# Order of work at the end of the second attention: sums, turned weights, loads of y and weight splits

## The chip, the cores and the metric

The kernel runs on one core of a Trainium2 chip. The metric is the device time of one execution in microseconds, median of three runs.

## The reference

A float32 stack of three layers over x of 512 tokens by 2048 features: a latent attention (mla, 16 heads), a sliding-window attention with sinks (swa, 32 query heads of 64, 4 key heads), and a stick-breaking attention beside a recurrence (stick). The change lies at the end of the second:

```python
proj = h @ w_in                       # q, k, v, gate
q, k = rope(q), rope(k)
s = where(valid, q k^T * D**-0.5, NEG_INF)      # own block of 128 keys and the one before
m = max(max(s), sink)
e = exp(s - m)
y = (e / (sum(e) + exp(sink - m))) @ v
x = x + (y * silu(gate)) @ w_out
```

Every large product is computed to nearly float32 precision: each operand is split into a high part (rounded, made by ScalarE) and a low part (the difference, made by VectorE or GpSimd), and PE sums high x high, high x low and low x high.

## The kernel before, in words

Tokens (512) stand in the free dimension, features in the 128 partitions. A weight tile is 2048 x 128 (1 MB), loaded by one DMA from SP's queue into one of two raw buffers, split in four pieces of 128 x 512 by `hi` (line 605, ScalarE) and `lo` (613, VectorE), and multiplied piece by piece by `multiply` (639 to 641, 12 matmuls a piece). `s_lo` counts pieces whose low part is made: a raw buffer is free for the next load when all four pieces of its tile are counted.

The phase swa runs 17 bodies. Body i projects the query tile and the gate tile of head pair i and does the attention of pair i - 1. Body 15 (`ends` in the code) still projects, body 16 (`not proj`) does only attention, and fills PE with the first tiles of the output projection out2: `early_output` (PE) multiplies piece p of tile (0, 0) and (0, 1) by turns, with chunks 4p to 4p + 3 of y as the other operand. The attention result of a pair leaves in two ways: for pairs up to 13 the turned weights go through a gather by DMA and are used a body later (`pv_prev`, "former pair"); bodies 15 and 16 turn the weights of their own pair on PE (`turn`, 1947 and 1951), copy them high (`turned_hi`, ScalarE) and low (`turned_lo`, VectorE, 658), and multiply (`pv`, 1981). Body 15 does both: the former pair's sums (`sum_prev`, 2196, counted as end_sum) must be out of a PSUM bank before `turn` may write it, and its `y_prev` and `y` share one buffer: `y` (2280) waits until the store of `y_prev` (732) has landed (`s_ystore`).

y goes to DRAM by one store a pair and comes back in four parts of up to four chunks (`load_y`, 741), each allowed once gate piece `part` of body 15 is multiplied. Then `y_hi` (1538, ScalarE) and `y_lo` (1548; VectorE, but chunks 4 to 7 GpSimd) split it. Chunk 15 is made in place by body 16's own `y`.

What sets the order around the change: each engine runs its instructions in the order in which `swa_T` (PE), `swa_A` (ScalarE), `swa_V` (VectorE), `swa_G` (GpSimd) and `attention_dmas` (SP) issue them; a wait blocks all behind it on that engine. The table `STEPS` (line 140 on) lists the counted steps of each engine, to turn a name into a semaphore value. In VectorE's body 15: maxima, inverse, this_lo(0), this_lo(1), q_cos, q_turn, q_sin, qr, this_lo(2), the four sums of the former pair, q_lo0, q_lo1, this_lo(3), y_prev, silu, the four low parts of the turned weights, next_lo(0), next_lo(1), sum_rows (2271), y, next_lo(2), next_lo(3). In body 16: y_lo 0 and 1, gate (2187), y_lo 2 and 3, first_lo(0), maxima (2161), inverse, first_lo(1), y_lo 8 to 11, first_lo(2), silu, turned_lo with first_lo(3) in their middle, y_lo 12 to 14, sum_rows, y, y_lo 15. this_lo is a piece of body 15's gate tile, next_lo one of out2's tile (0, 0), first_lo one of its tile (0, 1). SP's queue at the end of the phase: load tile (0, 0), load tile (0, 1) (when this_lo(3) is made), store y_prev, load y parts 0, 1, 2, store y of body 15, load tile (1, 0), y part 3, load tile (1, 1).

## Time and profile before

| | us |
|---|---|
| runs (3) | 2100.08, 2100.10, 2100.24; median 2100.1 |
| span of the profiled execution | 2098.9 |
| PE busy | 2082.9 (99%) |
| VectorE busy | 1417.7 (68%) |
| ScalarE busy | 996.4 (47%) |
| GpSimd busy | 191.2 (9%) |

The span runs from the first to the last instruction; the 1.2 us to the median lie around it. PE's clock was granted at 0.999 over the span. In all views PE is TensorE, DVE VectorE, ACT ScalarE, POOL GpSimd, SP the queue that issues the DMAs. Matmuls are pipelined, one of 512 columns starting every 0.23 us and listed with 0.39; an idle time is counted from the end of the one before. Consecutive operations of one kind are merged in a timeline (x4), and their time is then from the first start to the last end.

### The profile page before, as it was taken

To read this page: it belongs to the slowest core of one execution; us is meant where nothing else is said; L and a number is where in the kernel's file an instruction comes from. 1 tells how busy PE (TensorE), PEld (TensorE's weight loads), DVE (VectorE), ACT (ScalarE), POOL (GpSimd) and SP (SyncE) were. 2 spreads that over 40 slices of the span, in tenths; PEclk is the share of its full clock that TensorE was granted. 3 is DMA by queue.
4 is the path that set the end of the run, shared out by engine and by line. 5 is a ranking of instruction groups with operands and counts; after the bars stand their busy time and mean duration, and the time that the engine had idled before them with its cause. 6 is when DMAs were issued, how large, how long until landed. Compare 5 with 4: busy or idle time off the path is not lost. (4 is left out here: it accounts for less than half of the span.)

```text
span 2098.9 us, 30066 instructions
## 1 busy us (share of the span) xinstructions
PE 2082.9 (99%) x9702; PEld 1734.5 (83%) x9702; DVE 1417.7 (68%) x2581; ACT 996.4 (47%) x1928; POOL 191.2 (9%) x197
## 2 busy tenths in 40 slices
PE   9999999999999999999999999999999999999999
PEld 7888888888888888888888788888888888888887
DVE  6677777777733568888888633677777677868432
ACT  6444444445422446666666633544454545446221
POOL 0111111112101000000000122200000000003000
PEclk9999999999999999999999999999999999999999
DMA  7324444445733624444444734533434334345742
GB/s 227 100 72 113 111 112 114 113 114 170 210 83 97 196 63 122 126 127 127 127 127 118 250 95 115 170 106 86 121 101 133 87 108 119 109 114 156 218 112 70
DMA packets 409917, 264.40 MB, mean 126 GB/s; under 512 B 20480, under 2 KB 382720, under 8 KB 409856
## 3 DMA queue, kind: packets, MB, share of 16 engines
q1 hardware_dynamic: 401120, 255.87, 43.1%
q10 hardware_dynamic: 8736, 7.74, 1.5%
q8 instruction: 35, 0.57, 0.1%
q14 instruction: 26, 0.21, 0.0%
HBM read 210.33 MB, written 24.12 MB: 112 GB/s over the span
## 5 line engine op out<-in xcount | busy, mean ns | idle before, releaser
L639 PE MATMUL pp<-act_hi,w_hi 128*128 128x512 f32 x2304 | 903.1, 392 | 6.9 <-DVE w_lo L613 4.2
L641 PE MATMUL pp<-act_hi,w_lo 128*128 128x512 f32 x2304 | 898.2, 390 | 0.0
L640 PE MATMUL pp<-act_lo,w_hi 128*128 128x512 f32 x2304 | 897.9, 390 | 0.0
L613 DVE TENSOR_TENSOR w_lo<-raw,w_hi 128x512 fp32r<-128x512 f32 x680 | 457.1, 704 | 360.7 <-ACT w_hi L605 359.8
L605 ACT ACTIVATE w_hi<-raw 128x512 fp32r<-128x512 f32 (+1 forms) x684 | 396.2, 622 | 456.2 <-PE pp L641 231.3
L639 PEld LDWEIGHTS pp<-act_hi,w_hi 128*128 128x128 f32 x2304 | 433.1, 188 | 100.9 <-DVE w_lo L613 6.0
L641 PEld LDWEIGHTS pp<-act_hi,w_lo 128*128 128x128 f32 x2304 | 432.9, 188 | 91.1
L640 PEld LDWEIGHTS pp<-act_lo,w_hi 128*128 128x128 f32 x2304 | 433.2, 188 | 87.3 <-issue 0.2
L658 POOL TENSOR_TENSOR pT_lo<-gathered,pT_hi 128x640 fp32r<-128x640 f32 x30 | 46.5, 1571 | 358.9 <-ACT pT_hi L654 358.9
L1318 ACT ACTIVATE prob<-ps,minus,q_scale 128x512 f32<-128x512 f32 (+1 forms) x64 | 39.0, 615 | 78.3 <-DVE minus L1398 78.3
L639 PE MATMUL ps<-act_hi,w_hi 128*128 128x512 f32 x176 | 69.3, 394 | 0.0
L641 PE MATMUL ps<-act_hi,w_lo 128*128 128x512 f32 x176 | 68.5, 389 | 0.0
L640 PE MATMUL ps<-act_lo,w_hi 128*128 128x512 f32 x176 | 68.5, 389 | 0.0
L2045 ACT ACTIVATE s_prob<-ps,s_minus 128x256 f32<-128x256 f32 x96 | 44.7, 472 | 44.6 <-DVE s_minus L2161 44.6
L1705 POOL TENSOR_TENSOR acc<-acc,square 128x512 f32<-128x512 f32 x30 | 41.2, 1373 | 252.6 <-ACT square L1631 251.8
L1548 POOL TENSOR_TENSOR act_lo<-y_lru,act_hi 128x512 fp32r<-128x512 f32 x7 | 11.1, 1620 | 557.3 <-ACT act_hi L1538 557.3
L654 ACT ACTIVATE s_pT_hi<-gathered 128x1792 fp32r<-128x1792 f32 x14 | 23.9, 1705 | 72.2 <-DMA gathered<-turned 72.2
L2066 ACT ACTIVATE s_prob<-s_prob,s_inv 128x256 f32<-128x256 f32 x128 | 54.5, 503 | 0.0
L2161 DVE CUSTOM_DVE_ANT_0 ps<-ps,s_con,s_sink 128x256 f32<-128x256 f32 x96 | 47.4, 550 | 3.4 <-DVEq L2158 3.4
L1682 DVE TENSOR_TENSOR xT<-pp,xT 128x512 f32 (+1 forms) x28 | 19.3, 690 | 32.1 <-PE pp L641 32.1
L1901 DVE STREAM_TRANSPOSE turned<-s_prob 128x128 f32<-128x128 f32 (+1 forms) x56 | 32.8, 624 | 11.6 <-ACT s_prob L2066 11.6
L640 PEld LDWEIGHTS ps<-act_lo,w_hi 128*128 128x128 f32 x176 | 33.0, 188 | 7.3 <-issue 0.5
(435 smaller groups left out, 2755.1 us busy)
## 6 DMA issues: line engine op xcount, KB each, us to landing
raw<-w_in SPq DMA_DIRECT2D x48, 1024.0 KB, 5.9
raw<-swa_w_in SPq DMA_DIRECT2D x36, 1024.0 KB, 5.8
raw<-mla_w_in SPq DMA_DIRECT2D x23, 1024.0 KB, 5.7
raw<-mla_w_out SPq DMA_DIRECT2D x16, 1024.0 KB, 6.5
raw<-swa_w_out SPq DMA_DIRECT2D x16, 1024.0 KB, 6.1
raw<-w_out SPq DMA_DIRECT2D x16, 1024.0 KB, 6.9
gathered<-turned SPq DMA_DIRECT2D x224, 56.0 KB, 2.0
x_feature_major<-xT SPq DMA_DIRECT2D x8, 1024.0 KB, 9.7
```

Source lines behind the costliest of these rows:

```text
L605: q.eng.activation(dst, raw_piece(tile, p), ACT.Copy).then_inc(s_hi, tile.ups(p))
L613: q.eng.tensor_tensor(dst, raw_piece(tile, p), high, ALU.subtract).then_inc(s_lo, tile.ups(p))
L639: q.eng.matmul(psum[:, :], wh, ah, start=start and n == 0, stop=False)
L640: q.eng.matmul(psum[:, :], wh, al, start=False, stop=False)
L641: last = q.eng.matmul(psum[:, :], wl, ah, start=False, stop=stop and n == PIECE // P - 1)
L658: q.eng.tensor_tensor(out, in_, hi_part.bitcast(F32), ALU.subtract).then_inc(*q.did(step))
L1318: q.eng.activation(prob[:, OFF[b]:OFF[b] + w_], SCORE[b][:, 0:w_], ACT.Exp, bias=minus[:, b:b + 1], scale=q_scale[:, b:b + 1], accum_out=t ...
L1705: q.eng.tensor_tensor(into, into, src[:, k, :], ALU.add).then_inc(*q.did(f"sum{f}{k}"))
L1901: m = q.eng.transpose(out_, in_)
L2045: q.eng.activation(s_prob[:, h, b * 2 * P:(b + 1) * 2 * P], BANKS[h][half][:, b % 2 * 2 * P:(b % 2 + 1) * 2 * P], ACT.Exp, bias=s_minus[:, ...
L2066: m = q.eng.activation(pr, pr, ACT.Identity, scale=s_inv[:, h, b:b + 1])
L2161: m = q.eng.tensor_tensor_reduce(scores, scores, sc("band")[:, b * 2 * P - half * 2 * P:(b + 1) * 2 * P - half * 2 * P], s_q_scale[:, b:b ...
```

## The change

In body 15, VectorE makes the former pair's sums right behind the shuffle `q_turn`, then this_lo(2), q_sin and qr, then the four low parts of the turned weights (now counted as end_lo), then this_lo(3), and then the query's low parts, y_prev, silu, next_lo(0), sum_rows, y, next_lo(1). ScalarE copies the turned weights (end_hi) ahead of the query's high parts. Pieces 2 and 3 of tile (0, 0) are split in body 16: behind y_hi 1 on ScalarE and behind y_lo 1 on VectorE. In body 16 first_lo(1) goes ahead of inverse(1), and first_lo(3) behind all four low parts of the turned weights. SP loads y parts 0 and 1 ahead of tile (0, 1) and of the store of y_prev. The arithmetic, the number of instructions and the bodies 0 to 14 stay.

```diff
--- before.py
+++ after.py
@@ -139,10 +139,10 @@
     },
     "swa": {
         "T": "s00 s01 s10 s11 pv_prev0 pv_prev1 t00 t01 t10 t11 pv0 pv1".split(),
-        "A": ("exp00 exp01 exp02 exp03 sink0 exp10 exp11 exp12 exp13 sink1 norm0 norm1 tanh low_prev0 low_prev1 q_hi0 q_hi1 "
-              "turned_hi pt_hi00 pt_hi01 pt_hi10 pt_hi11 y_low0 y_low1").split(),
-        "V": ("gate ready0 minus00 minus01 ready1 minus10 minus11 sum0 inv0 lo_prev sum1 inv1 turned q_cos q_turn q_sin qr "
-              "end_sum00 end_sum01 end_sum10 end_sum11 q_lo0 q_lo1 sum_prev00 sum_prev01 sum_prev10 sum_prev11 y_prev silu pt_lo00 pt_lo01 pt_lo10 pt_lo11 "
+        "A": ("exp00 exp01 exp02 exp03 sink0 exp10 exp11 exp12 exp13 sink1 norm0 norm1 tanh low_prev0 low_prev1 "
+              "end_hi00 end_hi01 end_hi10 end_hi11 q_hi0 q_hi1 turned_hi pt_hi00 pt_hi01 pt_hi10 pt_hi11 y_low0 y_low1").split(),
+        "V": ("gate ready0 minus00 minus01 ready1 minus10 minus11 sum0 inv0 lo_prev sum1 inv1 turned q_cos q_turn "
+              "end_sum00 end_sum01 end_sum10 end_sum11 q_sin qr end_lo00 end_lo01 end_lo10 end_lo11 q_lo0 q_lo1 sum_prev00 sum_prev01 sum_prev10 sum_prev11 y_prev silu pt_lo00 pt_lo01 pt_lo10 pt_lo11 "
               "y_sum00 y_sum01 y_sum10 y_sum11 y").split(),
         "G": "sink keys pair".split(),
     },
@@ -772,10 +772,13 @@
             load_tile(q.eng, Tile(f"out{n}", 0, 0))
             if phase == "mla":
                 gather(units - 1)
+            else:
+                load_y(q, n, 0)
+                load_y(q, n, 1)
             load_tile(q.eng, Tile(f"out{n}", 0, 1))
             if phase == "swa":
                 store_y(q, phase, units - 1, units - 3, "V.y_prev")
-            for part in range(3):
+            for part in range(0 if phase == "mla" else 2, 3):
                 load_y(q, n, part)
             store_y(q, phase, units - 1, units - 2)
             if n == 1:
@@ -1970,7 +1973,7 @@
             def pv():
 
                 if not proj or ends:
-                    q.eng.wait_ge(*q.at("V.pt_lo11"))
+                    q.eng.wait_ge(*q.at("V.end_lo11" if ends else "V.pt_lo11"))
                     q.eng.wait_ge(*q.at("G.pair", i))
                     hi_, lo_ = (pT[:, :].rearrange("p (h n) -> p h n", h=2) for pT in (s_pT_hi, s_pT_lo))
                     for half, parts in enumerate((((0, 0, 0, 2), (1, 2, 1, 1)), ((2, 5, 0, 2), (1, 3, 0, 1), (3, 4, 1, 1)))):
@@ -2081,9 +2084,17 @@
             def turned_hi(h, half):
                 if not proj or ends:
                     q.eng.wait_ge(*q.at(f"T.t{h}{half}"))
-                    copy_hi(q, turned_blocks(s_pT_hi, h, half), TURNED[h][half][:, half * P:], f"pt_hi{h}{half}")
+                    copy_hi(q, turned_blocks(s_pT_hi, h, half), TURNED[h][half][:, half * P:], f"{'end' if ends else 'pt'}_hi{h}{half}")
+
+            def all_turned():
+                for h in range(2):
+                    for half in range(2):
+                        turned_hi(h, half)
             if not proj:
-                y_hi(q, 2, range(0, 4))
+                y_hi(q, 2, range(0, 2))
+                hi(q, Tile("out2", 0, 0), 2)
+                hi(q, Tile("out2", 0, 0), 3)
+                y_hi(q, 2, range(2, 4))
                 hi(q, Tile("out2", 0, 1), 0)
                 y_hi(q, 2, range(4, 8))
             weights(0, 0)
@@ -2110,23 +2121,20 @@
             this_hi(3)
             if not proj:
                 hi(q, Tile("out2", 0, 1), PIECES - 1)
+            if ends:
+                all_turned()
             if proj:
                 q.eng.wait_ge(*q.at("V.qr"))
                 copy_hi(q, s_q_a[0:HD2, :], s_q[0:HD2, :], "q_hi0")
                 copy_hi(q, s_q_b[HD2:P, :], s_q[HD2:P, :], "q_hi1", rest=not attn)
             if ends or not proj:
-                turned_hi(0, 0)
-                turned_hi(0, 1)
-                turned_hi(1, 0)
-                turned_hi(1, 1)
                 next_hi(0)
                 next_hi(1)
                 if not proj:
+                    all_turned()
                     y_hi(q, 2, range(12, KC - 1))
                 low_rows(0)
                 low_rows(1)
-                next_hi(2)
-                next_hi(3)
                 return
             next_hi(0)
             next_hi(1)
@@ -2172,14 +2180,17 @@
 
             def turned_lo(h, half):
                 if not proj or ends:
-                    q.eng.wait_ge(*q.at(f"A.pt_hi{h}{half}"))
+                    name = "end" if ends else "pt"
+                    q.eng.wait_ge(*q.at(f"A.{name}_hi{h}{half}"))
                     sub_lo(q, turned_blocks(s_pT_lo, h, half), TURNED[h][half][:, half * P:], turned_blocks(s_pT_hi, h, half),
-                           f"pt_lo{h}{half}")
+                           f"{name}_lo{h}{half}")
             def first_lo(p):
                 if not proj:
                     lo(q, Tile("out2", 0, 1), p)
             if not proj:
                 y_lo(q, 2, range(0, 2))
+                lo(q, Tile("out2", 0, 0), 2)
+                lo(q, Tile("out2", 0, 0), 3)
             if attn:
                 multiplied(q, Tile("swa", i - 1, 1))
                 if not isinstance(i, int) or i >= 2:
@@ -2204,8 +2215,8 @@
             if prev:
                 q.eng.wait_ge(*q.at("A.turned_hi", i - 1))
                 sub_lo(q, s_pT_lo[:, :], gathered[:, :], s_pT_hi[:, :], "lo_prev")
+            first_lo(1)
             inverse(1)
-            first_lo(1)
             if not proj:
                 y_lo(q, 2, range(8, 12))
             first_lo(2)
@@ -2225,21 +2236,30 @@
                     q.eng.wait_ge(*q.at("V.q_lo1", i - 1))
                 q.eng.tensor_tensor(s_q[:, :], pp[0][:, :], s_cos[:, :], ALU.mult).then_inc(*q.did("q_cos"))
                 q.eng.stream_shuffle(s_spin, pp[0][:, :], PARTNER).then_inc(*q.did("q_turn"))
+                if ends:
+                    sum_prev(0)
+                    sum_prev(1)
+                    this_lo(2)
                 q.eng.wait_ge(*q.at("V.q_turn"))
                 q.eng.tensor_tensor(s_spin, s_spin, s_sin[:, :], ALU.mult).then_inc(*q.did("q_sin"))
                 q.eng.wait_ge(*q.at("V.q_sin"))
                 q.eng.tensor_tensor(s_q[:, :], s_q[:, :], s_spin, ALU.add).then_inc(*q.did("qr"))
-            this_lo(2)
             if ends:
-                sum_prev(0)
-                sum_prev(1)
+                turned_lo(0, 0)
+                turned_lo(0, 1)
+                turned_lo(1, 0)
+                turned_lo(1, 1)
+                this_lo(3)
+            else:
+                this_lo(2)
             if proj:
                 q.eng.wait_ge(*q.at("A.q_hi0"))
                 sub_lo(q, s_q_a[HD2:P, :], s_q[0:HD2, :], s_q_a[0:HD2, :], "q_lo0")
                 q.eng.wait_ge(*q.at("A.q_hi1"))
                 q.eng.tensor_tensor(s_q_b[0:HD2, :], s_q[HD2:P, :], s_q_b[HD2:P, :].bitcast(F32),
                                     ALU.subtract).then_inc(*q.did("q_lo1", rest=not attn))
-            this_lo(3)
+            if not ends:
+                this_lo(3)
             if prev:
                 if not ends:
                     sum_prev(0)
@@ -2253,15 +2273,14 @@
                 q.eng.wait_ge(*q.at("A.tanh"))
                 q.eng.scalar_tensor_tensor(s_y[:, 1, :], s_th[:, :], 1.0, s_gate, ALU.add,
                                            ALU.mult).then_inc(*q.did("silu", rest=proj and not ends))
-            turned_lo(0, 0)
-            turned_lo(0, 1)
-            first_lo(3)
-            turned_lo(1, 0)
-            turned_lo(1, 1)
             if ends:
                 next_lo(0)
-                next_lo(1)
             if not proj:
+                turned_lo(0, 0)
+                turned_lo(0, 1)
+                turned_lo(1, 0)
+                turned_lo(1, 1)
+                first_lo(3)
                 y_lo(q, 2, range(12, KC - 1))
             def sum_rows(half):
                 if not proj or ends:
@@ -2279,9 +2298,11 @@
                 q.eng.wait_ge(*q.at("V.y_sum11"))
                 q.eng.scalar_tensor_tensor(s_y[:, 0, :] if proj else last_y, s_y_sum[:, :], 0.5, s_y[:, 1, :],
                                            ALU.mult, ALU.mult).then_inc(*q.did("y"))
-            if not ends:
-                next_lo(0)
+            if ends:
                 next_lo(1)
+                return
+            next_lo(0)
+            next_lo(1)
             next_lo(2)
             next_lo(3)
```

## Rows read from the trace of the kernel before

**Rows 1.** The page, engine shares: busy us (share of the span) xinstructions.

```profile
PE 2082.9 (99%) x9702; PEld 1734.5 (83%) x9702; DVE 1417.7 (68%) x2581; ACT 996.4 (47%) x1928; POOL 191.2 (9%) x197
```

**Rows 2.** Waits of PE, whole span: engine line <- waited for: total us, times, longest.

```profile
PE pp L639 <- DVE w_lo L613: 4.2, 4, 2.0
```

**Rows 3.** Timeline of PE, restarts: start us, us, operation, [idle before <-releaser].

```profile
1149.63 0.33 PE L1947 MATMUL pt<-con,s_prob 128*128 128x128 f32 x1 [1.10 <-DVE s_y_sum L2196]
...
1155.13 0.49 PE L1981 MATMUL po<-s_pT_hi,pair 128*128 128x512 f32 x1 [1.01 <-DVE s_pT_lo L658]
...
1163.46 0.47 PE L639 MATMUL pp<-act_hi,w_hi 128*128 128x512 f32 x1 [1.78 <-DVE act_lo L1548]
...
1167.58 0.47 PE L639 MATMUL pp<-act_hi,w_hi 128*128 128x512 f32 x1 [0.76 <-DVE w_lo L613]
...
1174.24 0.50 PE L639 MATMUL pp<-act_hi,w_hi 128*128 128x512 f32 x1 [0.97 <-DVE w_lo L613]
...
1183.35 0.50 PE L1981 MATMUL po<-s_pT_hi,pair 128*128 128x512 f32 x1 [0.39 <-DVE s_pT_lo L658]
...
1188.95 0.50 PE L639 MATMUL pp<-act_hi,w_hi 128*128 128x512 f32 x1 [0.28 <-DVE act_lo L1548]
```

**Rows 4.** Timeline of ACT, 1144 to 1152.

```profile
1144.91 1.08 ACT L2073 ACTIVATE s_y_low<-pt 64x512 f32<-64x512 f32 x2
...
1150.38 0.98 ACT L654 ACTIVATE s_pT_hi<-pt 128x512 fp32r<-128x512 f32 x2 [1.77 <-PE pt L1947]
```

**Rows 5.** Timeline of DVE, 1145 to 1160.

```profile
1145.10 0.74 DVE L2227 STREAM_SHUFFLE square<-pp 128x512 f32<-128x512 f32 x1
...
1147.82 1.75 DVE L2196 TENSOR_TENSOR s_y_sum<-pt,s_y_low 64x256 f32<-64x256 f32 x4
...
1150.92 0.70 DVE L613 TENSOR_TENSOR w_lo<-raw,w_hi 128x512 fp32r<-128x512 f32 x1
...
1152.86 1.15 DVE L658 TENSOR_TENSOR s_pT_lo<-pt,s_pT_hi 128x512 fp32r<-128x512 f32 x2
...
1157.70 0.87 DVE L2271 TENSOR_TENSOR s_y_sum<-ps,s_y_low 64x256 f32<-64x256 f32 x2
...
1158.67 0.69 DVE L2280 SCALAR_TENSOR_TENSOR s_y<-s_y_sum,s_y 128x512 f32<-128x512 f32 x1
...
1159.28 1.29 DVE L613 TENSOR_TENSOR w_lo<-raw,w_hi 128x512 fp32r<-128x512 f32 x2
```

**Rows 6.** DMA issues: xcount, KB each, us to landing; windows at 1151.6, 1152.2, 1153.5; whole span.

```profile
raw<-swa_w_out SPq DMA_DIRECT2D x1, 1024.0 KB, 6.2
...
y_feature_major<-s_y SPq DMA_DIRECT2D x1, 256.0 KB, 6.3
...
y_whole<-y_feature_major SPq DMA_DIRECT2D x1, 1024.0 KB, 8.4
...
y_feature_major<-y_out SPq DMA_DIRECT2D x15, 256.0 KB, 2.2
```

**Rows 7.** Timeline of POOL, 1165 to 1172.

```profile
1165.39 1.49 POOL L1548 TENSOR_TENSOR act_lo<-y_whole,act_hi 128x512 fp32r<-128x512 f32 x1 [21.41 <-ACT act_hi L1538]
...
1166.85 1.73 POOL L1548 TENSOR_TENSOR act_lo<-y_whole,act_hi 128x512 fp32r<-128x512 f32 x1
...
1171.03 0.39 POOL L2310 CAST pair<-s_v_hi 128x256 fp32r<-128x256 f32 x1
```

**Rows 8.** Timeline of DVE, 1165 to 1168 and at 1914.

```profile
1165.64 1.80 DVE L613 TENSOR_TENSOR w_lo<-raw,w_hi 128x512 fp32r<-128x512 f32 x1
...
1167.36 0.54 DVE L2161 CUSTOM_DVE_ANT_0 ps<-ps,s_con,s_sink 128x256 f32<-128x256 f32 x1
...
1914.36 2.89 DVE L613 TENSOR_TENSOR w_lo<-raw,w_hi 128x512 fp32r<-128x512 f32 x2
```

**Rows 9.** Timeline of ACT, 1173 to 1181.

```profile
1173.00 1.71 ACT L2066 ACTIVATE s_prob<-s_prob,s_inv 128x256 f32<-128x256 f32 x4
...
1179.85 0.97 ACT L654 ACTIVATE s_pT_hi<-pt 128x512 fp32r<-128x512 f32 x2
```

## The prediction, made before the changed kernel ran

> **What bounds the kernel now.** Read the page's engine shares first: PE (TensorE) is busy 2082.9 of 2098.9 us [rows 1], so all its idle time together is 16 us, and no edit of order can gain more. The list of waits by PE then says what ends that idle time: above all VectorE's low parts of weights, 4.2 us in 4 waits [rows 2]. The edit touches only the last attention unit with projections (I call it unit 15) and the drain after it (unit 16), so the third view is PE's timeline there: seven restarts between 1149.6 and 1189.0, whose marked idle times 1.10, 1.01, 1.78, 0.76, 0.97, 0.39 and 0.28 add up to 6.29 us [rows 3]. That is the ceiling: 0.30% of the time. A measurement of this kernel can tell about 0.2%, 4.2 us, from no change.
>
> Which of the seven can be had is not PE's affair. The last one, output chunk 15 at 1188.95 [rows 3], needs the drain's own attention result. Behind it lies a chain from VectorE's first maximum at 1167.36 [rows 8] over ScalarE, which is busy without a break from its normalisation at 1173.00 to the high parts at 1179.85 [rows 9], back to VectorE and PE. From the maximum to chunk 15 it is 1188.95 - 1167.36 = 21.6 us. PE's own work from its restart at 1167.58 to chunk 15 is 21.37 less the idle 0.97, 0.39 and 0.28, so 19.7 us [rows 3]. The chain is longer by 1.9 us or so: **the end follows the moment at which unit 16's maxima start on VectorE**, and stalls of PE after 1167 cost nothing by themselves. So the sum is the shift of that moment.
>
> **Part 1: sums ahead in unit 15.** The four sums (1.75 us [rows 5]) move from behind qr and a weight split to behind the shuffle, which ends at 1145.84 [rows 5]; the low rows that they read are there at 1144.91 + 1.08 = 1145.99 [rows 4] (the first about half of that earlier). They end near 1147.5, not 1149.57. PE wants the bank at 1149.63 - 1.10 = 1148.5 [rows 3]: the 1.10 go. What is late next: nothing until the product.
>
> **Part 2: turned weights ahead of the query's parts.** The turns finish 1.26 sooner (start 1148.4), ScalarE's four copies, which began at 1150.38 [rows 4], begin at 1149.1. Their four low parts need 2.2 us (first pair at 1152.86, 1.15 for two, the second pair alike [rows 5]), from 1149.7 to 1151.9; PE comes to the product at about 1153.0 (1155.13 - 1.01 - 1.10 [rows 3]). The 1.01 go. The cover has 1 us of room.
>
> What they are moved past pays: the weight split this_lo(3), ended at 1150.92 + 0.70 = 1151.62 [rows 5], now follows the four low parts: 1151.9 + 0.6 = 1152.5. The query's low parts (2 x 0.7), y_prev (0.7), silu (0.7) and next_lo(0) (0.6) follow: y_prev ends near 1154.55, next_lo(0) near 1155.9. The sums of the product (2 x 0.87 [rows 5]) end at 1157.6 instead of 1158.57. PE, after the product and the fourth gate piece and scores, is ready for output chunk 0 near 1159.5 (1163.46 - 1.78 - 2.11 [rows 3]).
>
> **Part 3: y's DMAs, and the wait that stays.** The two loads of y go out when gate pieces 0 and 1 are through (about 1145.9 and 1148.6) and land before 1155; one took 8.4 us only behind other transfers [rows 6]. The 1.78 us wait thus loses its cause. But SP's queue still holds, in this order, the tile load out2(0,1), which waits for this_lo(3), and the store of y_prev; and VectorE's "y" waits until that store has landed, since it overwrites its buffer. Before: the tile load went out as this_lo(3) ended, 1151.62, and took 6.2 us to land [rows 6]: 1157.8; the store, issued 0.6 later, took 6.3 [rows 6]: about 1158.5; y started at 1158.67 [rows 5], so this wait was already a tie with the sums. After: this_lo(3) ends 1152.5, the tile lands at 1152.55 + 6.2 = 1158.8, the store 0.7 later, 1159.5. **y starts at 1159.5, 0.8 later than before**, though its inputs are there at 1157.6. Behind y queue on VectorE next_lo(1), all of unit 16, and PE's chunks.
>
> What of the store's landing the trace doesn't settle: the same 256 KB with nothing ahead took 2.2 us (y_out, 15 of them [rows 6]), which would be 1156.8 and no wait; behind a tile it took 6.3. I take the latter, as the order in the queue is the same as in that row. The Trainium skill ("DMA: Bandwidth & Descriptors", Queues, rings and completion order) says the completion write lands only after every earlier write of that DMA engine; by it the 2.2 us is not to be had with the tile ahead, and the 0.7 us between the landings agrees.
>
> **Part 4: splits moved in the drain.** Between y's end (1160.2) and the maxima VectorE now has nine operations: next_lo(1), y_lo 0 and 1, splits 2 and 3 of out2(0,0), gate, y_lo 2 and 3, first_lo(0). At 0.6 each (two take 1.29 [rows 5]) the maxima would start at 1160.1 + 5.4 = 1165.5, a gain of 1.85. But **GpSimd** runs y_lo 4 to 7 meanwhile. In the trace of before its first (1.49 us from 1165.39) held up w_lo, which then took 1.80 instead of 0.69, and w_lo its second, 1.73 instead of 1.49; the operation on PSUM after it took 0.54 [rows 7, 8]. At 1914 two w_lo beside such work took 2.89 instead of 1.29 [rows 8]. So they take turns: each w_lo or y_lo waits for GpSimd's operation and the other way round, a pair costing about 1.7 us where VectorE alone needs 0.6. In before, ScalarE's y_hi 4 came so late that only one VectorE operation met this (1.11). Now y_hi 4 follows hi(out2(0,1), 0), which waits for the tile at 1158.8; GpSimd begins at about 1160.05, just as y ends, and four VectorE operations meet its four: next_lo(1), y_lo 0, y_lo 1, split 2, each +1.1. The first of its two casts (0.39 each [rows 7]) delays split 3 by some 0.3. Sum 4 x 1.1 + 0.3 = 4.7: maxima at 1165.5 + 4.7 = 1170.2. Chunk 0 on PE at 1163.7 (before 1163.46), chunks 2 and 3 only near 1169.2, the next tile at 1170.5.
>
> **Ends of that price.** Below: no turns at all, 0, if GpSimd is the one that waits. Above: all eight port-using operations held, 8 x 1.1 = 8.9, which four GpSimd operations can't do. I take 4.7, by the count of meetings. The Trainium skill ("SBUF — State Buffer", SBUF: two separate sides) says whoever starts first holds the pair for the whole instruction and a VectorE operation is concerned when it has two SBUF inputs. It doesn't say who is next when both queue; read as "a running VectorE queue keeps it" the time would be that of rival B. The rows at 1165 and 1914 speak for turns.
>
> **first_lo(1) ahead of inverse(1)** takes PE's 0.97 stall away, first_lo(3) behind the four low parts most of the 0.39: both lie beside the 21.6 us chain, so 0. The cover is the chain itself; if the maxima came 2 us sooner relative to PE, they would count. next_hi(2), (3) move into ScalarE's idle time. The split 2, 3 later delay the tile load of out2(1,0) to near 1167.9; it is needed after 1188.
>
> **Sum.** Maxima 1170.2 - 1167.36 = +2.8 us, and 21.6 us behind them unchanged: chunk 15 at 1191.8. Span 2098.9 + 2.8 = 2101.7. Before, the median 2100.1 is 1.2 above the span; so 2102.9 us, 0.13% more.
>
> **Rivals.** A is this forecast, chance 0.62 (2101.5 to 2104.2 by half a microsecond either way at the landing and one meeting more or less).
> B, faster: VectorE is not held. Maxima at 1165.5, 2098.3 us. For it: an operation can slip between two of GpSimd's; against it the turns at 1165 and 1914 [rows 7, 8]. 0.20.
> C, slower for sure: the tile out2(0,1) lands later because the two loads of y stand ahead of it in the queue. A load of the same size behind two others took 8.4 us to land where the tile took 6.2 [rows 6]: 2.2 more. Everything behind y then shifts by that on top of the 2.8: 2105.1. It passes +4.2 once the tile lands 1.4 later than I put it, after 1160.2. Against: the second load is issued 4 us ahead. 0.10.
> D: the store lands in time. Then y at 1157.7, two or three operations get ahead of GpSimd, the rest meet it: maxima near 1167.9, 2100.6 us. 0.05.
> E: the edit does more than I count, as where neither the wait nor the turns bite: y at 1157.7 and 5.4 us behind it, maxima at 1163.7, 2096.4. 0.03.
>
> **Numbers.** Range 2097.8 to 2104.6: B to the upper end of A, leaving out C and E, 0.15 or so. Faster by over 0.2% (below 2095.9): 0.03. Slower (above 2104.3): 0.12. Within: 0.85.
>
> **What would show it.** After: no idle ahead of the first turn and the first product in unit 15; y_whole landed before 1155; y's start 0.1 us behind the landing of the y_prev store and the sums' end 2 us before; w_lo and y_lo of 1.1 to 1.8 us just behind y, beside GpSimd's 1.7; maxima near 1170. Wrong if y starts at 1157.7, if these VectorE operations last 0.69, or if the distance from maxima to chunk 15 is not 21.6.

## The result, and the profile after

| | before | after |
|---|---|---|
| median of nine runs each, us | 2100.24 (2099.43 to 2101.05) | 2105.16 (2104.12 to 2108.72) |
| ratio to before | | 1.0024, 95% interval 1.0015 to 1.0032 |
| span of the profiled execution | 2098.9 | 2102.3 (its time 2104.12, the lowest of the nine) |

The changed kernel is slower by 4.9 us. The forecast was 2.8 us slower, and the time lies 0.6 us above the range. A second set of eleven runs (last experiment) gave 2104.89, 3.8 us above its own runs of before, so the size is 3.8 to 4.9 us.

The page, engine shares of after: busy us (share of the span) xinstructions.

```profile
PE 2084.9 (99%) x9702; PEld 1736.4 (83%) x9702; DVE 1420.5 (68%) x2581; ACT 995.3 (47%) x1928; POOL 192.4 (9%) x197
```

PE is *busy* for 2.0 us longer than in [rows 1] with the same 9702 matmuls, and VectorE for 2.8 us longer with the same 2581 instructions. Neither engine got work. Both facts belong to the answer: matmuls at a lower clock, and subtractions held up by GpSimd's. A third part of it, VectorE's wait for a store, is idle time and shows in neither.

Waits of PE in after, whole span: engine line <- waited for: total us, times, longest.

```profile
PE pp L639 <- DVE act_lo L1551: 7.8, 3, 5.7
PE pp L639 <- DVE w_lo L613: 2.4, 2, 1.9
```

The waits for w_lo fell from the 4.2 of [rows 2] to 2.4, as intended. A wait of 5.7 us for the low part of y stands in their place. Timeline of PE in after, the restarts: start us, us, operation, [idle before <-releaser].

```profile
1147.41 0.60 PE L1950 MATMUL pt<-con,s_prob 128*128 128x128 f32 x4
...
1151.68 0.39 PE L1984 MATMUL po<-s_pT_hi,pair 128*128 128x512 f32 x1
...
1163.83 0.77 PE L639 MATMUL pp<-act_hi,w_hi 128*128 128x512 f32 x1 [5.73 <-DVE act_lo L1551]
...
1168.22 0.80 PE L639 MATMUL pp<-act_hi,w_hi 128*128 128x512 f32 x1 [1.16 <-DVE act_lo L1551]
...
1185.87 0.50 PE L1984 MATMUL po<-s_pT_hi,pair 128*128 128x512 f32 x1 [0.16 <-DVE s_pT_lo L658]
...
1192.06 0.50 PE L639 MATMUL pp<-act_hi,w_hi 128*128 128x512 f32 x1 [0.90 <-DVE act_lo L1551]
```

The first turn and the first product no longer wait: the 1.10 and 1.01 of [rows 3] are gone. But output chunk 0 waits 5.73, and the matmul behind it lasts 0.77 instead of 0.47.

To compare absolute times of two traces, a common mark is needed. I take the shuffle of unit 15, which in before starts at 1145.10 [rows 5]. Timeline of VectorE in after:

```profile
1144.14 0.73 DVE L2238 STREAM_SHUFFLE square<-pp 128x512 f32<-128x512 f32 x1
...
1159.12 1.23 DVE L2299 SCALAR_TENSOR_TENSOR s_y<-s_y_sum,s_y 128x512 f32<-128x512 f32 x1 [2.46 <-DMA y_feature_major<-s_y]
1160.27 1.75 DVE L613 TENSOR_TENSOR w_lo<-raw,w_hi 128x512 fp32r<-128x512 f32 x1
1161.94 3.42 DVE L1551 TENSOR_TENSOR act_lo<-y_whole,act_hi 128x512 fp32r<-128x512 f32 x2
1165.28 1.68 DVE L613 TENSOR_TENSOR w_lo<-raw,w_hi 128x512 fp32r<-128x512 f32 x2
...
1169.29 0.54 DVE L2169 CUSTOM_DVE_ANT_0 ps<-ps,s_con,s_sink 128x256 f32<-128x256 f32 x1
```

and of POOL in the same stretch:

```profile
1158.53 6.28 POOL L1551 TENSOR_TENSOR act_lo<-y_whole,act_hi 128x512 fp32r<-128x512 f32 x4 [15.52 <-ACT act_hi L1541]
1164.76 0.85 POOL L2331 CAST pair<-s_v_hi 128x256 fp32r<-128x256 f32 x1
```

After's clock stands 0.96 us earlier than before's at the mark, so after's maxima at 1169.29 are 1170.25 in the time of before. y waited 2.46 us until the store of y_prev had landed, and then ran against GpSimd: y 1.23, next_lo(1) 1.75, two y_lo 3.42 together.

DMA issues of after, 1144.5 to 1161: xcount, KB each, median us to landing.

```profile
y_whole<-y_feature_major SPq DMA_DIRECT2D x3, 1024.0 KB, 5.5
raw<-swa_w_out SPq DMA_DIRECT2D x1, 1024.0 KB, 5.8
```

The first two loads of y, issued at 1144.92 and 1147.67, land at 1150.37 and 1153.20, well ahead of any need. The tile goes out at 1151.52 and lands at 1157.28; the store goes out at 1153.68 and lands at 1159.09.

The last view shows what I had not looked for. Windows of before and then of after: us, busy time and instructions of each engine, PEclk the granted clock, DMA share, GB/s.

```profile
1160.00:1165.00 5.00, 3.22 (x21) 2.53 (x19) 2.94 (x5) 3.04 (x6) 0.00 (x0) 1.00 1.04 387
1165.00:1170.00 5.00, 4.15 (x18) 3.09 (x18) 4.82 (x12) 3.42 (x11) 4.61 (x4) 1.00 1.05 311
```

```profile
1155.00:1160.00 5.00, 3.10 (x22) 2.70 (x20) 2.45 (x5) 4.91 (x10) 1.47 (x2) 1.00 1.03 346
1160.00:1165.00 5.00, 1.17 (x3) 0.83 (x3) 5.00 (x4) 0.01 (x1) 5.00 (x4) 0.72 0.16 62
1165.00:1170.00 5.00, 3.84 (x9) 2.33 (x8) 5.00 (x10) 0.00 (x0) 1.42 (x2) 0.50 0.29 82
1170.00:1175.00 5.00, 5.00 (x18) 3.97 (x17) 4.06 (x17) 4.61 (x20) 0.00 (x0) 0.76 0.92 286
```

PE's clock, 1.00 in every one of these windows before, fell to 0.50, that is from 2.4 to 1.2 GHz, while PE idled ahead of chunk 0. It stayed there for (0.28 + 0.50 + 0.24) x 2 x 5 = 10.2 us. The next view shows it in the matmuls: they start 0.43 apart instead of 0.23.

```profile
1168.81 0.63 PE L640 MATMUL pp<-act_lo,w_hi 128*128 128x512 f32 x1
1169.23 0.63 PE L641 MATMUL pp<-act_hi,w_lo 128*128 128x512 f32 x1
```

Fifteen of them start 0.43 instead of 0.23 apart. The first six cost nothing, as PE waited 1.16 us for the low part of y behind them anyway; the nine from 1168.22 on put PE 9 x 0.2 = 1.8 us further behind. It then came late with the second turn of unit 16, on which ScalarE and, behind it, VectorE wait. ACT timeline of after at 1184:

```profile
1184.03 0.98 ACT L654 ACTIVATE s_pT_hi<-ps 128x512 fp32r<-128x512 f32 x2 [1.29 <-PE ps L1950]
```

and the DVE timeline behind it:

```profile
1184.65 1.16 DVE L658 TENSOR_TENSOR s_pT_lo<-ps,s_pT_hi 128x512 fp32r<-128x512 f32 x2 [1.10 <-ACT s_pT_hi L654]
```

From the maxima to chunk 15 it is 1192.06 - 1169.29 = 22.8 us, not 21.6.

**Where the time went, profiled run against profiled run.** Maxima later against the mark: (1169.29 - 1144.14) - (1167.36 - 1145.10) = 2.9 us. Chain behind them: 22.77 - 21.59 = 1.2. Rest of the span behind chunk 15: (2102.3 - 1192.06) - (2098.9 - 1188.95) = 0.3. Together 4.4. Up to the mark after was 0.96 faster, in code that the change doesn't touch, so the spans differ by 3.4 only. The medians, where such offsets wash out, differ by 4.9.

### The profile page after: what moved, and what is told of

It is laid out like the page before. It is cut to its first block, busy times and chain, and to the rows that moved or that the text cites. A ratio compares the mean times of both kernels' runs of the same rounds, so it can differ in the third digit from the quotient of the medians.

```text
span 2102.3 us, 30095 instructions
## 1 busy us (share of the span) xinstructions
PE 2084.9 (99%) x9702; PEld 1736.4 (83%) x9702; DVE 1420.5 (68%) x2581; ACT 995.3 (47%) x1928; POOL 192.4 (9%) x197
## 4 chain that ended last, share of the span: by engine, by line
PE 93%; DVE 4%; ACT 1%; DMA 1%; issue 1%; ACTq 0%; SPq 0%; DVEq 0%
PE pp L639 25%; PE pp L640 25%; PE pp L641 25%; PE ps L639 2%; PE ps L641 2%; PE ps L640 2%; PE ps L662 2%; PE ps L664 2%; PE ps L663 2%; DVE w_lo L613 1%; PE po L662 1%; PE po L664 1%; PE po L663 1%; PE pt L1967 1%; PE pt L1969 1%
```

## The experiments

All but two start from the changed kernel. They are told in the order of what they settle. The following table is read from their traces: y's start and the maxima's are counted from the shuffle; "shift" is (maxima plus chain) against before's 43.85; the last column is worked out from windows as above; "time" is the median against the runs of before beside it. Four kernels (both of these, loads of y back, loads of y alone, sums and turned weights alone) ran on another chip than the other six, beside runs of before with a median of 2100.47; the others stood beside 2100.91, or 2101.09 for splits back and after again. So across these groups the differences from before are the ones to compare.

| kernel | y | maxima | chain to chunk 15 | shift | time | us at 1.2 GHz near chunk 0 |
|---|---|---|---|---|---|---|
| before | 13.57 | 22.26 | 21.59 | | | 0 |
| after | 14.98 | 25.15 | 22.77 | +4.1 | +4.9 | 10.2 |
| after again | 15.96 | 26.29 | 22.30 | +4.7 | +3.8 | 10.2 |
| y in a buffer of its own | 12.55 | 21.71 | 21.58 | -0.6 | +0.5 | 3.4 |
| GpSimd later | 14.62 | 20.64 | 21.62 | -1.6 | -1.0 | 0 |
| both of these | 12.51 | 18.54 | 21.59 | -3.7 | -4.0 | 0 |
| store ahead of the tile | 12.57 | 18.59 | 21.63 | -3.6 | -3.5 | 0 |
| PE filled | 14.60 | 25.37 | 21.62 | +3.1 | +4.8 | 0 |
| loads of y back | 14.60 | 23.85 | 21.59 | +1.6 | +2.5 | 3.4 |
| loads of y alone | 14.63 | 23.82 | 21.59 | +1.6 | -0.2 | 0 |
| sums and turned weights alone | 14.52 | 22.57 | 21.59 | +0.3 | +0.6 | 6.8 |
| splits back | 14.96 | 24.73 | 21.60 | +2.5 | +2.7 | 6.8 |

A shift is that of one execution and a time that of a whole set. The profiled executions of own buffer, GpSimd later and PE filled were the lowest of their sets, that of loads alone the second highest; there the two columns part by 0.6 to 1.8 us.

### The wait alone: y in a buffer of its own

```diff
-                if proj:
-                    q.eng.wait_ge(s_ystore, 16 * (H1 - 1 + i))
...
-                q.eng.scalar_tensor_tensor(s_y[:, 0, :] if proj else last_y, ...
+                q.eng.scalar_tensor_tensor(s_q[:, :] if proj else last_y, ...
```

The store of this y reads s_q too.

> The changed kernel, but unit 15's y goes to a buffer of its own (the query's, free by then), so it doesn't wait until the store of y_prev has landed. Theory (the wait and the turns with GpSimd set the maxima, the end follows them): y starts at about 1156.7 instead of 1159.1, two more VectorE operations get ahead of GpSimd, the maxima start near 1166.9 instead of 1169.3, time 2105.2 - 2.4 = 2102.8 us, and 1.2 less again if TensorE's clock stays at 2.4 GHz. Rival (the lower clock of TensorE after its idle time is what costs, VectorE's delays are covered): the maxima move but the time stays within 1 us of 2105.2 as long as the clock falls. Rival (the wait is a tie that other work covers): no change.

Measured: 2101.45 (2099.50 to 2103.42), ratio 1.0004 (0.9995 to 1.0013): no difference from before can be told any more, and it is 3.7 us below after. y starts with its inputs at 1156.98, and six of the nine operations behind it get through before GpSimd begins at 1161.03. DVE timeline of this kernel:

```profile
1156.98 0.69 DVE L2298 SCALAR_TENSOR_TENSOR s_q<-s_y_sum,s_y 128x512 f32<-128x512 f32 x1
...
1161.20 3.33 DVE L1552 TENSOR_TENSOR act_lo<-y_whole,act_hi 128x512 fp32r<-128x512 f32 x2
1164.46 1.76 DVE L613 TENSOR_TENSOR w_lo<-raw,w_hi 128x512 fp32r<-128x512 f32 x1
```

and its POOL timeline:

```profile
1161.03 6.33 POOL L1552 TENSOR_TENSOR act_lo<-y_whole,act_hi 128x512 fp32r<-128x512 f32 x4 [17.71 <-ACT act_hi L1542]
```

So the wait was real and 2.4 us long, and the last three operations are still held. That only three are held is in part due to this execution, the lowest of its eleven: the tile took 8.0 us to land here, 5.8 in after, and GpSimd, which starts behind it, began 2.2 us later against the mark. With a sooner tile more of them would meet GpSimd; the median, 2.0 us above this execution, fits that but has no trace.

### The turns alone: GpSimd later

```diff
             if not proj:
+                q.eng.wait_ge(*q.at("V.ready0"))
                 y_lo(q, 2, Y_GPSIMD[2])
```

> The changed kernel with one wait more: GpSimd's four y_lo begin only when VectorE has come to unit 16's maxima. Theory (turns at the shared port cost 4.7 us): y and the eight operations behind it last 0.69 each, the maxima start 6.0 us behind y, near 1165.1 instead of 1169.3, chunk 15 follows 21.6 behind; time 2105.2 - 5.4 = 2099.8 us, or 2101.0 if the clock still falls. Rival (the turns are covered by PE's lower clock or by DMAs): less than 1 us faster. Rival (GpSimd's chunks 4 to 7 are then late for PE): a new idle time ahead of them, over 1 us.

Measured: 2099.91 (2098.10 to 2102.33), ratio 0.9998 (0.9989 to 1.0007), 5.3 us below after and 0.1 from the theory's 2099.8. y still waits for its store, but all behind it runs undisturbed. DVE timeline of this kernel:

```profile
1158.73 0.69 DVE L2299 SCALAR_TENSOR_TENSOR s_y<-s_y_sum,s_y 128x512 f32<-128x512 f32 x1 [2.15 <-DMA y_feature_major<-s_y]
1159.34 0.68 DVE L613 TENSOR_TENSOR w_lo<-raw,w_hi 128x512 fp32r<-128x512 f32 x1
1159.94 1.29 DVE L1551 TENSOR_TENSOR act_lo<-y_whole,act_hi 128x512 fp32r<-128x512 f32 x2
...
1164.75 0.55 DVE L2169 CUSTOM_DVE_ANT_0 ps<-ps,s_con,s_sink 128x256 f32<-128x256 f32 x1
```

From y to the maxima it is 1164.75 - 1158.73 = 6.02 us for ten operations; in after the same ten took 1169.29 - 1159.12 = 10.17. The turns cost 4.15 us. PE's idle ahead of chunk 0 was 2.75 and the clock stayed at 2.4 GHz.

### Both: own buffer and GpSimd later

The two diffs above in one kernel.

> The changed kernel with both: unit 15's y in a buffer of its own (no wait for the store) and GpSimd's four y_lo held until VectorE has come to the maxima. Theory (wait and turns are all that delays the maxima): y starts at about 1157 as its sums are there, the maxima 6.0 us behind it, near 1163, chunk 15 another 21.6 behind; 2.0 us faster than with either alone, 2097.9 us. Rival (with the maxima so early something else ends the stretch, the tile's landing at 1159 ahead of first_lo(0) or PE's own 19.7 us): maxima near 1163 but less than 1 us gained over the kernel with GpSimd held alone.

Measured: 2096.46 (2096.08 to 2098.23), ratio 0.9982 (0.9973 to 0.9991). It is 4.0 us below its before; after was 3.8 to 4.9 above, so taking both causes away is worth 7.8 to 8.9 us. That is 1.4 us better than the theory had: it built on the median of GpSimd later, which lies 1.8 us above the execution with the trace. The maxima come 18.54 after the mark, 6.6 sooner than in after: 2.5 from y's start and 4.15 from the turns. For the maxima, the two causes add up and leave nothing over.

### One line of SP's order: store ahead of the tile

```diff
                 load_y(q, n, 1)
+                store_y(q, phase, units - 1, units - 3, "V.y_prev")
             load_tile(q.eng, Tile(f"out{n}", 0, 1))
-            if phase == "swa":
-                store_y(q, phase, units - 1, units - 3, "V.y_prev")
```

> The changed kernel with the store of y_prev ahead of the load of tile (0, 1) in SP's queue. Theory (the store lands late only because the tile stands ahead of it): it lands in 2.2 us, y starts near 1156.7 as soon as its sums are there; the tile lands 2.2 us later, which also holds GpSimd back until 1160.8; maxima near 1166.0 instead of 1169.3, time 2105.2 - 3.3 = 2101.9 us, 2100.7 if the clock stays up. Rival (a store takes 5 to 6 us by itself): y still at 1159, the tile later, time 2105 to 2107. Rival (PE then lacks tile (0, 1)): idle time ahead of its first piece, no gain.

Measured: 2097.38 (2096.74 to 2098.55), ratio 0.9984 (0.9975 to 0.9993): it beats both kernels too, and lies 3.3 us below the better of the two times that the theory allowed. The theory had GpSimd held back only until 1160.8 and most of the turns still there. DMA issues of this kernel, window at 1154.8 to 1155.5:

```profile
raw<-swa_w_out SPq DMA_DIRECT2D x1, 1024.0 KB, 7.0
y_feature_major<-s_y SPq DMA_DIRECT2D x1, 256.0 KB, 3.0
```

The store lands in 3.0 us instead of 5.4, so y doesn't wait. The tile goes out 2.5 us later against the mark, takes 7.0 us instead of 5.8 and lands at 1162.36; GpSimd, which needs it by way of ScalarE, begins only at 1163.61, when VectorE is in its last operation ahead of the maxima. DVE timeline:

```profile
1157.99 0.69 DVE L2298 SCALAR_TENSOR_TENSOR s_y<-s_y_sum,s_y 128x512 f32<-128x512 f32 x1
...
1163.41 0.69 DVE L613 TENSOR_TENSOR w_lo<-raw,w_hi 128x512 fp32r<-128x512 f32 x1
```

POOL timeline:

```profile
1163.61 5.41 POOL L1550 TENSOR_TENSOR act_lo<-y_whole,act_hi 128x512 fp32r<-128x512 f32 x4 [19.37 <-ACT act_hi L1540]
```

One move takes away both costs. It also shows how they were coupled. GpSimd begins 1.25 us after the tile's landing (1158.53 against 1157.28 in after, 1163.61 against 1162.36 here, 1161.03 against 1159.77 with the own buffer), and y 0.03 after the store's. Behind one another in SP's queue, tile and store land within 2 us of each other, so **the same two landings release VectorE and GpSimd together**. The Trainium skill ("DMA: Bandwidth & Descriptors", Queues, rings and completion order) has a completion land only after every earlier write of its DMA engine; 5.4 us behind the tile and 3.0 ahead of it agree with that.

### The clock alone: PE filled

```diff
             scores(1, 1)
+            if not proj:
+                for _ in range(24):
+                    q.eng.matmul(pp[0][:, :], s_q_a[:, 0:P], pairk_hi[:, :], start=True, stop=True)
```

> The changed kernel with 24 matmuls more, whose results nothing uses, on PE between unit 16's scores and output chunk 0, where PE was idle for 5.7 us; they need 5.5 us. Theory (the clock's fall costs the 1.2 us by which chunk 15 came later behind the maxima than 21.6): if the clock stays at 2.4 GHz, maxima unchanged near 1169.3, chunk 15 at maxima + 21.6 instead of 22.8, time 2104.0 us. Rival (the clock costs all that PE's slower matmuls add, 15 of them at 0.43 instead of 0.23 us): 3 us faster, 2102.2. Rival (the clock falls anyway, by the pauses between the chunks): no change.

Measured: 2105.69 (2103.05 to 2108.00, eight runs), ratio 1.0025 (1.0014 to 1.0035). The matmuls only keep PE at work between the scores and chunk 0. Windows of the profiled execution:

```profile
1160.00:1165.00 5.00, 4.50 (x20) 3.44 (x19) 5.00 (x4) 0.64 (x2) 5.00 (x4) 1.00 0.21 80
1165.00:1170.00 5.00, 2.50 (x11) 1.41 (x10) 5.00 (x7) 0.00 (x0) 2.15 (x3) 1.00 0.13 34
```

The maxima, on VectorE:

```profile
1170.02 0.54 DVE L2172 CUSTOM_DVE_ANT_0 ps<-ps,s_con,s_sink 128x256 f32<-128x256 f32 x1
```

and the last two restarts of PE:

```profile
1185.45 0.50 PE L1984 MATMUL po<-s_pT_hi,pair 128*128 128x512 f32 x1 [0.97 <-DVE s_pT_lo L658]
...
1191.64 0.50 PE L639 MATMUL pp<-act_hi,w_hi 128*128 128x512 f32 x1 [0.88 <-DVE act_lo L1551]
```

The clock was 1.00 throughout and the chain from maxima to chunk 15 back at 21.62 us, although the maxima came as late as in after. In this execution that ties the extra 1.2 us to the clock. The median does not bear it out: the theory had 2104.0, and it did not fall. The two executions with a mean clock of 1.000 took 2103.05 and 2103.67; the six with 0.997 to 0.999 took 2105.20 to 2108.00. The filler may thus have failed to hold the clock in most executions. That isn't shown: only one has a trace, a mean over the span doesn't say where the clock fell, and runs of before have 0.998 to 1.000 too. The split by clock agrees in sign with the trace, though its 3 us are more than 1.2.

### Loads of y back behind the tile and the store

```diff
             load_tile(q.eng, Tile(f"out{n}", 0, 0))
-            else:
-                load_y(q, n, 0)
-                load_y(q, n, 1)
             load_tile(q.eng, Tile(f"out{n}", 0, 1))
-            for part in range(0 if phase == "mla" else 2, 3):
+            for part in range(3):
```

> The changed kernel with SP's queue as before: both loads of y behind the tile and the store. Theory (the maxima are set by the store's landing and the turns, not by y's loads): the first load of y lands at 1162 to 1163 instead of 1151, so ScalarE's y_hi 0 and VectorE's y_lo 0 wait until then; next_lo(1) is out of the way by then and GpSimd starts near 1166, so that one or two VectorE operations meet it instead of four: y_lo 0 near 1163.5, maxima near 1169.5, time 2105 within 1 us. Rival (the loads of y were the gain of the change): 2 us slower or more, 2107. Rival (they do harm, as they bring GpSimd into VectorE's stretch): faster than 2104.

Measured: 2102.94 (2101.65 to 2105.10), ratio 1.0014 (1.0005 to 1.0023). This was a miss for my theory, which gave the loads no part in the slowdown. With them back, VectorE waits 2.04 us for y instead of for GpSimd, GpSimd begins only at 1166.47 and holds one operation. DVE timeline:

```profile
1162.78 1.29 DVE L1548 TENSOR_TENSOR act_lo<-y_whole,act_hi 128x512 fp32r<-128x512 f32 x2 [2.04 <-ACT act_hi L1538]
...
1167.00 1.79 DVE L613 TENSOR_TENSOR w_lo<-raw,w_hi 128x512 fp32r<-128x512 f32 x1
```

The loads sooner thus take away a 2 us wait and open the door for a 4 us one: they are 1.3 to 2.4 us of the slowdown, by letting GpSimd start with y.

### Loads of y alone, on the kernel before

```diff
             load_tile(q.eng, Tile(f"out{n}", 0, 0))
+            else:
+                load_y(q, n, 0)
+                load_y(q, n, 1)
             load_tile(q.eng, Tile(f"out{n}", 0, 1))
...
-            for part in range(3):
+            for part in range(0 if phase == "mla" else 2, 3):
```

> The kernel before with only SP's queue changed as in the change: the two loads of y ahead of the tile and the store. Theory: y_lo 0 no longer waits for its load (idle 2.1 us on VectorE gone), GpSimd starts near 1162 and meets y_lo 2, y_lo 3 and first_lo(0) instead of first_lo(0) alone (2.2 us more); the maxima start 1 us sooner to 1 us later than in the kernel before, time 2100.1 +- 1. Rival (sooner loads are a plain gain): 2 us faster. Rival (turns eat more than the wait gives): 1 to 3 us slower.

Measured: 2100.31 (2099.21 to 2103.05), ratio 1.0001 (0.9992 to 1.0010). In the profiled execution, one of the slower (its time was 2102.77), GpSimd began at 1161.86 and held four operations, and the tile took 7.4 us to land; SP took 3.43 us to issue the store of y_prev, where 0.36 is usual, and it landed 7.5 us after its issue. SP timeline:

```profile
1152.20 3.43 SPq L732 DMA_DIRECT2D y_feature_major<-s_y  x1
```

Seven of the eleven runs lie below 2101, so most executions probably didn't look like this one. Alone the loads make no difference that the interval, 1.9 us either way, can tell; their harm comes with the other edits.

### Sums and turned weights alone, on the kernel before

```diff
+                if ends:
+                    sum_prev(0)
+                    sum_prev(1)
+                    this_lo(2)
                 q.eng.wait_ge(*q.at("V.q_turn"))
...
+            if ends:
+                turned_lo(0, 0)
+                turned_lo(0, 1)
+                turned_lo(1, 0)
+                turned_lo(1, 1)
+                this_lo(3)
```

and end_hi on ScalarE, as in the change; SP's order and the splits as before.

> The kernel before with only the sums of the former pair and the turned weights of unit 15 moved ahead; SP's queue and all weight splits of out2 as before. Theory (this_lo(3) ends 0.9 us later, and with it the tile's and the store's landings, y and the loads of y behind them): PE's idle times of 1.10 and 1.01 us go, but the maxima come 0.9 us later, time 0.9 us slower than before. Rival (PE's idle times are what counts): 2.1 us faster. Rival (the wait for the store doesn't move): no change.

Measured: 2101.10 (2100.52 to 2104.53), ratio 1.0006 (0.9997 to 1.0015), +0.6 us where parts 1 to 3 of the prediction gave +0.9. PE timeline of this kernel, ahead of chunk 0:

```profile
1163.01 0.76 PE L639 MATMUL pp<-act_hi,w_hi 128*128 128x512 f32 x1 [4.34 <-DVE act_lo L1548]
```

The 2.1 us won ahead of the turn and the product reappear as idle ahead of chunk 0 (1.78 before [rows 3], 4.34 here), and the clock was at 1.2 GHz for 6.8 us. It still cost nothing in the chain, 21.59.

### Splits back

```diff
-                y_hi(q, 2, range(0, 2))
-                hi(q, Tile("out2", 0, 0), 2)
-                hi(q, Tile("out2", 0, 0), 3)
-                y_hi(q, 2, range(2, 4))
+                y_hi(q, 2, range(0, 4))
```

and likewise in VectorE's list, with first_lo(1) and first_lo(3) where they were.

> The changed kernel with its weight splits where they were before: pieces 2 and 3 of out2(0,0) at the end of body 15, first_lo(1) behind inverse(1), first_lo(3) in the middle of the turned weights. Sums, turned weights and the loads of y stay as changed. Theory: the harm comes from GpSimd's four subtractions beginning with y, and they are released by the tile out2(0,1) on ScalarE, not by these splits; VectorE has the same nine operations between y and the maxima. So GpSimd begins within 0.5 us of y, four operations of VectorE last 1.7 us, maxima to chunk 15 is 21.6 us if the clock holds and up to 22.8 if PE's idle ahead of chunk 0 (longer here, as three pieces stand ahead of y_lo 0 on VectorE) lets it fall: 2104.5 to 2106 us. Rival: the moved splits are what pushes VectorE late; without the moves it is near the kernel with the sums and turned weights alone, 2101 to 2102 us.

Measured: 2103.75 (2102.57 to 2104.94), ratio 1.0012 (1.0003 to 1.0021), between the two theories: 0.75 us below mine and 1.75 above the rival's. GpSimd did begin with y (1159.19 and 1159.36). The moved splits are worth 1.1 to 2.3 us of the slowdown, against none in my theory. PE's idle ahead of chunk 0 was longest of all here. PE timeline:

```profile
1166.16 0.77 PE L639 MATMUL pp<-act_hi,w_hi 128*128 128x512 f32 x1 [7.36 <-DVE act_lo L1551]
```

and two windows, with the clock:

```profile
1160.00:1165.00 5.00, 0.00 (x0) 0.00 (x0) 5.00 (x4) 0.67 (x2) 5.00 (x4) 0.79 0.21 79
1165.00:1170.00 5.00, 3.84 (x10) 3.06 (x11) 5.00 (x9) 0.00 (x0) 2.07 (x3) 0.53 0.91 251
```

The low clock ended here at about 1169.7, 0.6 us behind the maxima at 1169.13; the chain is 21.60. In after it lasted 3.1 us past the maxima, and the chain grew by 1.2; in the second profile of after 2.1 us past them, and it grew by 0.7. Half speed hurts as far as it reaches into the time in which PE must catch up with the chain.

### The changed kernel once more

> The changed kernel itself, once more, for a second profiled execution and more times. Theory: y again within 0.5 us of the store's landing, GpSimd within 0.7 us of y, four VectorE operations of 1.7 us, maxima near 1169.3, the granted clock at 0.5 for some microseconds after PE's idle of over 5 us, maxima to chunk 15 over 22 us; median 2105.2, within 0.8. Rival: the profiled low clock of 10.2 us was a single case and the next execution shows 21.6 us; then the median stays at 2105 all the same and the clock is not part of it.

Measured: 2104.89 (2103.79 to 2106.63), ratio 1.0021 (1.0012 to 1.0030). The profiled execution took 2106.34, 2.2 us above the first one. DVE timeline:

```profile
1161.82 0.69 DVE L2299 SCALAR_TENSOR_TENSOR s_y<-s_y_sum,s_y 128x512 f32<-128x512 f32 x1 [3.48 <-DMA y_feature_major<-s_y]
1162.43 0.68 DVE L613 TENSOR_TENSOR w_lo<-raw,w_hi 128x512 fp32r<-128x512 f32 x1
1163.03 3.44 DVE L1551 TENSOR_TENSOR act_lo<-y_whole,act_hi 128x512 fp32r<-128x512 f32 x2
1166.40 3.43 DVE L613 TENSOR_TENSOR w_lo<-raw,w_hi 128x512 fp32r<-128x512 f32 x2
```

and the DMA issue of the tile:

```profile
raw<-swa_w_out SPq DMA_DIRECT2D x1, 1024.0 KB, 8.0
```

Here the tile took 8.0 us to land, not 5.8, and y started 1.0 later against the mark. Of the 4.7 us by which chunk 15 shifted here, 4.0 lie in the maxima and 0.7 in the chain. Among the profiled kernels with the loads of y and the tile in after's order, the tile took 5.8 to 6.2 us in five and 7.4 to 8.0 in three (own buffer, loads alone and this one); in the three with the loads behind it, 6.0 to 6.2. So this is rival C, in some executions only.

## Why the prediction was wrong

**Right.** The sums and the turned weights did what parts 1 and 2 say. The wait for the store of y_prev took over (y 0.03 us behind the landing, in both profiles), and VectorE and GpSimd took turns. The maxima stood at +2.9 us; the forecast was +2.8. The tests took each of the two causes away alone and together. Each set against its own before, and these against after's +3.8 to +4.9, the wait is worth 3.3 to 4.4 us, the turns 4.8 to 5.9 and both 7.8 to 8.9. So these two are shown, not only argued.

**Right by two errors that cancel.** In the time of before, y started at 1159.12 + 0.96 = 1160.1, not 1159.5. The failed step is "the store 0.7 later" than the tile. I took the distance of the two landings from before, where the issues were 0.6 apart. After the change y_prev is done later and they are 2.2 apart, and the landings 1.8. The prediction itself had y_prev end at 1154.55, 2.0 us behind its issue of the tile, and didn't use it. The tile landed 0.6 sooner than forecast, which hid part of that. Against that the turns cost 4.15, not 4.7: GpSimd started before y, so y took one of the four meetings, at +0.5 only. That the maxima came out at +2.8 and +2.9 was luck; in the second profile they came at +4.0.

**Wrong: "stalls of PE after 1167 cost nothing by themselves".** This is the step that failed in both profiles of after. It compared PE's work (19.7 us) with the chain (21.6) and kept 1.9 us of slack, at full clock. The change lengthened the idle ahead of chunk 0 to 5.7 us. PE's clock then fell to 1.2 GHz for 10.2 us, its matmuls ate the slack, and the chain took 22.8: +1.2 us (+0.7 in the second profile). The slack that could take up a delay was also smaller than 1.9. With the clock up (PE filled) the idle times of that stretch are 0.97 ahead of the product and 0.88 ahead of chunk 15. In after they are 0.16 and 0.90: only the first shrank, since the second waits for what VectorE makes of the product itself. Of the 1.9 us that PE's work took longer from its restart ahead of the maxima (22.8 instead of 20.8 us without the idle times) 0.8 was covered and 1.2 came through, within 0.1. My own text had the numbers for the idle: it put chunk 0 at 1163.7 and PE's readiness at 1159.5, 4 us apart, and never asked what an idle of that size does. In [rows 3] nothing is longer than 1.78, and there the clock never fell. The evidence for this step is three traces (both of after, and PE filled); no median shows it, as filling PE did not lower the time.

**Wrong: rival C as an either-or.** Its 2.2 us came true in size (8.0 against 5.8) but in some executions only. Where it did, in the second profile, y started 1.0 later and the maxima term was 1.2 us too small, more than the chain's 0.7. That the median lies 1 us above the first profiled execution, the lowest of its nine, fits this, but is only argued: just two executions have a trace. Why the tile takes 2 us longer in some executions and not in others wasn't settled: the loads of y ahead of it are a condition by the rows above, not yet a cause.

**Not in the sum.** Behind chunk 15 the profiled spans differ by another 0.3 us. And the base: I put 1.2 us around the span, median against the span of one execution. Time less span is 1.8 in a run (2104.12 - 2102.3), so the profiled execution of before probably lay 0.6 above the median itself.

**The gain that was missed.** Rival E had 2096.4 for the case that neither the wait nor the turns bite. The kernel with both taken away came to 2096.46, with its maxima at 18.54 from the mark, which is 1163.6 in the time of before; rival E had 1163.7. The edit was sound, and what spoiled it were two things that it triggered on other engines.

## What to carry to other kernels

Work moved forward on the critical engine is won only if what it frees next is not held by the same things: list, for each engine, what the next release is, and check whether two engines that hold each other up, as VectorE and GpSimd do here, are released by neighbouring landings. A small store on which an engine waits goes ahead of a large load in the queue, if the load has room: here one line gave 7.5 to 7.8 us, part of it because the later load also held GpSimd back. And count slack of PE with the clock that it will have: here each idle of 4.3 us or more ahead of chunk 0 brought the clock down, and the slow matmuls behind it can take away the slack that made the idle look harmless.

## What was not expected of the hardware

- PE's clock fell after idles of 4.3 to 7.4 us (for 3.4, 6.8 or 10.2 us) and stayed at 2.4 GHz after 2.75 followed by 1.29. The length of the low stretch did not follow that of the idle: 7.36 gave 6.8 us, 5.73 gave 10.2, 4.80 gave 3.4. The Trainium skill ("TensorE: Matmul & The Clock Gate", What's actually happening) says that the clock has just two levels and falls on idleness; the 0.43 and 0.23 us between matmuls agree.
- The profile of the own-buffer kernel shows 3.4 us at 1.2 GHz though no idle of PE above 2.3 us stands there. That is not explained.
- GpSimd's casts, 0.39 us alone [rows 7], took 0.85 beside VectorE's subtractions, and y, a scalar_tensor_tensor, met GpSimd in the same way as the subtractions (1.23 in after, 1.64 with the splits back, 0.69 alone).
- Issuing one DMA took SP 3.43 us instead of 0.36 in one execution (loads alone), with two loads of 1 MB in flight. Why isn't known.
